# First attention of a two-block transformer kernel: where TensorE's scores stand within a step

## The reference

```
p_cmp = masked_softmax(q @ k_cmp, cmp_end <= t)          # 31 compressed keys
o_cmp = p_cmp @ v_cmp
p_sel = masked_softmax(q @ k_sel, pos <= t)              # 16 blocks chosen of 8 that exist: all of them
o_sel = p_sel @ v_sel
p_win = masked_softmax(q @ k_win, wmask)                 # window of 512 = the whole sequence
o_win = p_win @ v_win
o = g0 * o_cmp + g1 * o_sel + g2 * o_win
y = o @ w_out
```

## Time and profile before

| what | value |
|---|---|
| median of 3 runs | 2070.02 us (2069.49 to 2073.59) |
| the profiled execution | 2071.35 us, its span 2069.6 us |
| PE busy | 1890.6 us, 91% of the span |
| DVE, ACT, POOL busy | 42%, 35%, 40% |
| first attention, from the transposes of part 0 to those of part 101 (of 0 to 103) | 169.95 us of the span (174.99 to 344.94) |
| PE's share of the chain that ended last | 79% |

### The profile page before, as it was taken

The page is one execution under the profiler, slowest core; times in us unless marked ns, Lnnn a source line. Parts: engine busy times, 40 slices in busy tenths (PEclk is TensorE's granted clock), DMA queues, the critical chain, the costliest instruction groups (busy, mean ns, idle before and its releaser), DMA issues.

```text
span 2069.6 us, 24011 instructions
## 1 busy us (share of the span) xinstructions
PE 1890.6 (91%) x8890; PEld 1519.0 (73%) x8890; DVE 877.8 (42%) x1316; ACT 720.8 (35%) x1147; POOL 822.4 (40%) x413
## 2 busy tenths in 40 slices
PE   5899999899879999997799869999898899999986
PEld 4786767678768888885668438877786688888865
DVE  5236776681453312358720460016455521022147
ACT  5446776133232222222233332235321332133132
POOL 3244656373034454455134143460043334444441
PEclk9999999999999999998899889999999999999998
DMA  4321000242012233224022102220022122222321
GB/s 147 108 102 41 1 1 28 96 143 102 13 69 102 88 115 122 101 101 142 31 74 99 41 0 81 102 83 20 11 101 78 65 102 101 88 95 102 101 95 48
DMA packets 24117, 162.44 MB, mean 78 GB/s; under 512 B 2800, under 2 KB 3312, under 8 KB 4976
## 3 DMA queue, kind: packets, MB, share of 16 engines
q1 hardware_dynamic: 23040, 159.39, 21.9%
q10 hardware_dynamic: 1008, 2.12, 0.3%
HBM read 159.40 MB, written 2.10 MB: 78 GB/s over the span
## 4 chain that ended last, share of the span: by engine, by line
PE 79%; DVE 11%; ACT 3%; POOL 3%; issue 3%; DMA 1%; DVEq 0%; SPq 0%; ACTq 0%; POOLq 0%
PE psum L440 77%; PE psum L699 2%; DVE sqt L1431 1%; POOL w_lo L2053 1%; POOL q_st L2089 1%; DVE rstd L1446 1%; DMA ring<-in_panels 1%; ACT w_hi_r L974 1%; DVE o_acc L1504 1%; DVE acc L1433 1%; DVE sqt L1857 1%; ACT spare L1345 1%; DVE tmp L1469 0%; DVE rstd L1865 0%; DVE negmax L1902 0%
## 5 line engine op out<-in xcount | busy, mean ns | idle before, releaser
L2053 POOL TENSOR_TENSOR w_lo<-ring,w_hi_r 128x2048 fp32r<-128x2048 f32 x142 | 658.9, 4641 | 1009.0 <-ACT w_hi_r L974 1008.9
L440 PE MATMUL psum<-h_hi,w_hi_r 128*128 128x512 f32 x1264 | 500.9, 396 | 45.6 <-DVE h_lo L1462 31.9
L440 PE MATMUL psum<-h_lo,w_hi_r 128*128 128x512 f32 x1264 | 498.0, 394 | 0.0
L440 PE MATMUL psum<-h_hi,w_lo 128*128 128x512 f32 x1264 | 497.1, 393 | 0.0
L440 PE MATMUL psum<-big_r,w_hi_r 128*128 128x512 f32 (+1 forms) x1440 | 434.8, 385 | 24.3 <-DVE xt L1741 8.9
L974 ACT CAST w_hi_r<-ring 128x2048 fp32r<-128x2048 f32 x144 | 274.6, 1908 | 499.2 <-PE psum L440 492.6
L440 PEld LDWEIGHTS psum<-big_r,w_hi_r 128*128 128x128 f32 x1440 | 270.3, 192 | 80.4 <-issue 26.7
L440 PEld LDWEIGHTS psum<-h_hi,w_hi_r 128*128 128x128 f32 x1264 | 241.2, 191 | 106.1 <-issue 52.1
L440 PEld LDWEIGHTS psum<-h_hi,w_lo 128*128 128x128 f32 x1264 | 241.0, 191 | 51.0
L440 PEld LDWEIGHTS psum<-h_lo,w_hi_r 128*128 128x128 f32 x1264 | 241.0, 191 | 50.3 <-issue 0.5
L440 PE MATMUL psum<-big_r,w_lo 128*128 128x512 f32 (+1 forms) x720 | 276.5, 384 | 0.0
(11 more groups left out here) (274 smaller groups left out, 2259.4 us busy)
## 6 DMA issues: line engine op xcount, KB each, us to landing
ring<-in_panels SPq DMA_DIRECT2D x148, 1024.0 KB, 4.8
xt<-in_x SPq DMA_DIRECT2D x4, 512.0 KB, 6.4
out<-big SPq DMA_DIRECT2D x8, 256.0 KB, 2.1
big<-in_mem ACTq DMA_DIRECT2D x1, 1024.0 KB, 4.9
q_st<-in_ple ACTq DMA_DIRECT2D x1, 512.0 KB, 3.4
spare<-in_w_gate ACTq DMA_DIRECT2D x1, 192.0 KB, 6.2
spare<-in_w_k ACTq DMA_DIRECT2D x1, 128.0 KB, 8.7
params<-in_params ACTq DMA_DIRECT2D x1, 114.0 KB, 4.8
```

The costliest lines, as they stand in the source:

```text
L440: return nc.tensor.matmul(o, l, r, start=start, stop=stop, **kw)
L2053: g.tensor_tensor(w_lo[:, p], ring[:, p], plain(w_hi[:, p]), ALU.subtract).then_inc(lo_done[j], 1)
```

## The change

Within a step of the first attention, TensorE's list is put in another order. The scores of part `k + 3` stood first; now they stand after the transposes of part `k` and the products that are due. Nothing is added or removed, and no other engine's list changes.

```
             for k in STEPS:
-                if 0 <= k + 3 < NW:
-                    nsa_score(parts[k + 3])
                 if 0 <= k < NW:
                     nsa_turn(parts[k])
                 for n, kt in products_at.get(k, ()):
                     nsa_product(n, kt)
+                if 0 <= k + 3 < NW:
+                    nsa_score(parts[k + 3])
             pe.wait_ge(ns["probs"], NW)
```

## The result

| what | before | after |
|---|---|---|
| median, 6 runs each | 2069.76 us (2068.23 to 2073.59) | 2108.15 us over all six, 2107.99 us (2107.08 to 2110.23) over five of them |
| the profiled execution, its span | 2071.35, 2069.6 us | 2110.23, 2108.4 us |
| first attention, transposes of part 0 to those of part 103 | 173.94 us (174.99 to 348.93) | 214.46 us (172.70 to 387.16) |

One run after, of 3284.24 us, had a mean granted clock of 0.575 and is in no comparison. The ratio is 1.0179 with a 95% interval of 1.0168 to 1.019: the change costs 38 us (38.4 by the medians, 37 by the ratio), where 35 were forecast. The two profiled attentions differ by 40.5; that of the kernel after began 2.3 us earlier, and 38.2 of the spans' difference of 38.8 are accounted for with that.

What follows compares the result with a forecast made beforehand. TensorE's own list was taken to bound the attention (PE busy 164.88 of 169.95 us). Unit losses of 17.9 us in the first pair and 17.3 in the second gave 35, so 2070 + 35 = 2105 us, range 2088 to 2126.

Steps and rivals of the forecast that it cites:

- The bound: First attention: TensorE's own list bounds it, PE busy for 164.88 of 169.95 us, the other engines just ahead.
- the condition: T(k+2) begins no sooner than T(k) + L + 0.16 + answer: two plain 512-key steps need 3.32 us against 2.88.
- The walk: Start times of each unit's transposes computed part by part from the condition; second 512-key unit 16.97 us, before 13.99.
- POOL's store: Second 256-key unit: store of a finished pair (0.61 + 1.29) stands ahead of the compressed part's scaling, 1.5 of +2.5 us.
- the sum: Losses of all units of the attention added up: 17.9 us for the first pair, 17.3 for the second, 35 us.
- PE's busy time: In the attention after the change: stays about the same 165 us, of then 204 us.
- through two different parts: The chain's maximum belongs to part k+3, reciprocal and scaling to k+2, waiting only because DVE takes its list in order.
- the answer: From the end of S(k+3) to the start of T(k+2): 1.72 us in plain 512-key steps, 2.75 for a compressed part.
- No difference: Rival: same cyclic order on PE, whose busy time stays the bound if looseness is larger: 2070 us; 4 in 100.
- faster: Rival: T(k) no longer stands behind 0.53 us of scores, winning at most PE's idle 5.1 us: 2065; 3 in 100.
- Only the compressed parts count: Rival: plain steps keep 1.44 us, only the jump at 16 compressed parts costs, 1.2 each: 2089 us; 11 in 100.
- The clock swings: Rival: PE's waits drop the granted clock once in each of 16 units, some 26 us more: 2131; 12 in 100.

Runs made afterwards that it cites:

- E: Changed kernel, GpSimd scaling all but compressed parts by the raw row sum, their reciprocal left out (output not the reference's): 2099.30 us, ratio 1.0147.
- F: As E, and VectorE takes a compressed part's sum and reciprocal ahead of the next part's maximum: 2089.97 us, ratio 1.0088.
- K: As F, and ScalarE takes the high part of k ahead of the exponential of k+2: 2100.60 us, ratio 1.0144.
- H: Changed kernel, with a compressed part's sum and reciprocal ahead of the next part's maximum on VectorE: 2099.35 us, ratio 1.0142.
- A: Kernel before, with the scores moved only behind the transposes of their step, not behind the products: 2093.09 us, ratio 1.0107.
- D: Kernel before, with the scores of part k+4 instead of k+3 first in step k: 2072.20 us, ratio 0.9996.

## Why the prediction was right, and where it was off

**The bound and the condition held.** Two plain steps wanted 3.32 us; where two stand side by side (from 187.65 to 191.02) they take 1.88 and 1.49, together 3.37. The walk through the second 512-key unit came to 16.97 and the trace has 17.22, with transposes at 0, 1.88, 3.76, 5.55, 8.15, 9.61, 11.50, 14.08 and 15.83 against 0, 1.67, 3.59, 5.33, 7.97, 9.45, 11.33, 13.88 and 15.63. What I didn't foresee is that they are uneven: the condition ties T(k+2) to T(k), so an uneven first pair stays uneven, and PE waits at every second step for 0.3 or 0.7 us, not at each for 0.2. The two 384-key units took 15.79 and 15.97 (forecast 15.67 and 15.78), the 256-key units 11.00 and 13.08 (10.73 and 12.81). POOL's store stood where it was put:

```profile
253.00 0.61 POOL L2098 CAST big_r<-o_acc 128x512 fp32r<-128x512 f32 x1
253.70 1.30 POOL L2100 TENSOR_TENSOR big_r<-o_acc,big_r 128x512 fp32r<-128x512 f32 x1
254.99 2.53 POOL L2089 TENSOR_SCALAR q_st<-q_st,coef,gates 128x31 f32<-128x31 f32 x6
```

The transposes behind it, at 256.51, had idled for 1.29. But those ahead of it waited for something that the sum doesn't have, a low part, as did their counterparts of the second pair; these 2.3 us are the only waits of PE for anything but the scaling:

```profile
253.45 0.63 PE L699 MATMUL psum<-ident,q_st 128*128 128x128 f32 x4 [1.14 <-DVE h_lo L1678]
```

**What was too small, and where the sum was lucky.** In the five units the change costs 13.2 us where the walk gave 12.1, and in their four counterparts of the second pair (302.03 to 362.00) 10.4 where it gave 9.6. With the clock at 1.00 in both kernels, this tests the sum by itself: 23.6 for 21.7, too small by a tenth. The remaining 16.9 us lie in the other seven units, for which it had 13.5, among them the pair of 128-key units (16.64 where the walk gave 15.13, before 11.37) and the first 512-key units (2.6 and 3.0, that is 21.31 less 18.33, where I took 2). There the clock comes in: half of the time at 1.2 GHz is 5.1 us before and 11.7 after, so up to 6.6 of the 40.5 are clock, for which the sum had nothing. If it is all of that, the walk of those units was 3 us too high, and the two errors hid each other; the runs don't separate them. That the timed loss was 38 and not 40.5 goes with the start, 2.3 us earlier in that execution.

**PE's busy time was forecast wrong.** It should have stayed as it was; it rose by 15.6 us. In the five units it rose by 3.23 (58.89 to 62.12) with the clock at 1.00, and there the trace shows from what: the last matmul of the scores used to run on under the next transposes, for 0.16 us, and is exposed whenever these wait. That overlap sums to 5.31 us at 33 places before and to 2.08 at 13 after. Over the attention it falls by 7.5 us; with up to 6.1 us of busy time from the clock, 2 us stay open.

**What "through two different parts" was worth.** The prediction described the answer as a chain that passes from one part to another by DVE's order. E and F cut that tie: half of the loss went, 21.0 of 40.5. I expected the whole. The waits of F name what comes next: a second way, through ACT's and DVE's queues to the low part that frees a bank, with little slack of its own, and the scaling, which now waits for a late exponential of its own part. In the five units F's PE waits 2.6 us for the one and 2.9 for the other (before 0 and 0.9). The forecast came out since it used the tightest of these; it misjudged the remedies. K, which was to remove the second way, didn't, so how the 19.5 us that F still loses in the attention divide between the two stays open.

**The rivals.** *No difference* and *faster* are out by the ratio's interval. *Only the compressed parts count* is out by plain steps of 1.88 and 1.49 instead of 1.44, and by H: with the compressed part's jump cut from 2.60 to 1.70, 27.7 of the 40.5 us remain, and 10.6 of the 13.2 in the five units. *The clock swings* came in small. It was to be low in each of 16 units; it was low in these stretches of 4 us (columns as in the stretches above), and besides in the first 8 us of the attention, at 280 to 288 and at 292 to 296, where the kernel before has 176 to 184 and the 4 us around's slow step:

```profile
268.00:272.00 4.00, 4.00 (x25) 3.61 (x24) 0.66 (x3) 1.69 (x6) 2.38 (x6) 0.61 0.00 0
...
364.00:368.00 4.00, 3.55 (x16) 3.10 (x17) 2.19 (x6) 1.49 (x5) 3.34 (x7) 0.57 0.00 0
...
384.00:388.00 4.00, 2.95 (x12) 1.93 (x11) 1.96 (x4) 3.29 (x10) 3.91 (x10) 0.61 0.75 262
```

Stretches near 0.6 held a part at 1.2 GHz; the long runs of units with PE busy for 86% in short pieces (14.88 of 17.22) stayed at 1.00, 2.4 GHz. The Trainium skill, "TensorE: Matmul & The Clock Gate", section "A second HAM failure mode: psum-queue depth-cycling", tells of a kernel in which frequent small idles between groups of matmuls made the clock swing. The trace agrees for a few units only, with 0.95 over the attention against 0.97 before.

## What to carry to other kernels

When a loop over several in-order queues is full on one engine, write the condition that ties a step to the one before the last (end of the producer, plus every operation that stands in the way in any queue, other parts' included) and compare it with that engine's work in the same steps; the difference is the slack, and moving a block behind the others of its step spends a whole step of it (here 1.44 us against a slack of 1.00). Count the short steps too, as A shows: two steps of which one has less work hold less. Look for a second chain with nearly the same length before promising what a remedy gives: here cutting the tightest one brought back only half. And where a short operation waits in line behind one that waits for the busy engine, moving it ahead only at the part with the long answer gained 0.24 to 0.36%, while moving it everywhere gained nothing, most likely as it closed another loop.

## What the runs showed of the hardware

In the kernel after, the granted clock was low in the 4 us behind each of two light stretches, 268 to 272 (0.61) and 292 to 296 (0.59):

```profile
264.00:268.00 4.00, 2.83 (x27) 2.61 (x27) 3.10 (x7) 2.99 (x16) 2.53 (x7) 1.00 0.00 0
...
288.00:292.00 4.00, 2.38 (x14) 1.54 (x14) 3.76 (x9) 2.96 (x8) 3.09 (x7) 1.00 0.01 2
```

But the lightest such stretch, in the 256-key unit ahead of them, passed at 1.00 and was followed by 1.00:

```profile
252.00:256.00 4.00, 2.07 (x15) 1.60 (x14) 3.56 (x9) 2.13 (x8) 3.92 (x7) 1.00 0.02 6
256.00:260.00 4.00, 3.49 (x31) 3.32 (x32) 1.36 (x4) 2.07 (x8) 1.88 (x5) 1.00 0.00 0
```

And A and H, slower than before by 19 and 28 us in the attention, were granted 0.99 there, more than the kernel before: how often the clock falls doesn't simply follow how much PE waits. So kernels are best compared over stretches with the same clock: D is 1.0 us shorter than the kernel before over the attention and 0.6 longer in the five units.
